# The mixer's output projection in 512-wide pieces by token halves, and cross queries moved around the memory's keys and values

## The chip, the cores and the metric

The kernel runs on one core of one Trainium2 chip. The metric is the device time of one execution in microseconds. Five engines work beside each other, each through its own list of instructions in order: TensorE (PE; PEld is its weight load), VectorE (DVE), ScalarE (ACT), GpSimd (POOL) and SyncE (SP), which here only starts transfers. They order themselves against each other by semaphores.

## What is computed

One layer of an encoder on 1024 tokens of width 1024. Three mixers (windowed attention, differential attention, a bidirectional recurrence) give one tile of 1024 features; what follows them is the part that the change touches:

```python
x = x + jnp.concatenate([o_win, o_diff, o_rwkv], axis=-1) @ w_out[l]
x = x + cross_attn(rmsnorm(x, norm_cross[l]), mem_n, x_wq[l], x_wkv[l], x_wo[l])
...
def cross_attn(h, mem_n, wq, wkv, wo):
    q = (h @ wq).reshape(b, t, X_HEADS, X_HEAD_DIM)
    kv = (mem_n @ wkv).reshape(b, m, 2, X_HEADS, X_HEAD_DIM)
    s = jnp.einsum('bqhd,bkhd->bhqk', q, kv[:, :, 0]).astype(f32) * (X_HEAD_DIM ** -0.5)
    p = jax.nn.softmax(s, axis=-1)
    o = jnp.einsum('bhqk,bkhd->bqhd', p.astype(h.dtype), kv[:, :, 1])...
    return o @ wo
```

`mem_n` is the normed memory of 256 tokens, there are 4 heads of 128, and a SwiGLU block of width 2816 and a last norm follow.

## The kernel before

Every large product is made of three matmuls on split operands: activations are kept as a rounded part HH and a rest HL, weights as WH and WL, and HH·WH, HH·WL and HL·WH are summed in PSUM.

**The weight pipeline.** Weights come in pieces of 256 KB, numbered through the whole kernel (`pieces`). SP loads piece p into one of three RAW buffers once piece p-3 has been read out; ACT rounds it to WH (`hi`, L590), POOL makes WL (`lo`, L428), and PE takes it (`take`). There are six WH/WL slots, so ACT may round piece p only when PE has finished piece p-6 (`w_used`). ACT has `hi(upto)` calls between its other work, and these calls set how far ahead of PE it gets. A piece is either 256 rows by 256 columns (`slab`) or 128 rows by 512 columns (`wide_slab`). One piece of `w_out` as a `slab` feeds 48 matmuls with 256 moving columns.

**The stage in question** is the list `jobs2` on PE: four jobs of the output projection (`wout`, each 256 output columns for all 1024 tokens, with the token tiles as stationary operand, `token_job` L1545 and following), four of the memory's keys and values (`wkv`, on the 256 memory tokens), two of the queries (`wq`, 256 features each for all tokens, `feature_job`, lines L1540 to L1543). PSUM has eight banks and the jobs take banks 0-3 and 4-7 in turn; before job j PE waits for the evacuation of job j-2.

- Ahead of job 0 the recurrence's last steps are still running; `out_ready` weaves them in between the pieces of job 0. When the mixer's tile is done (`p_y`), SP loads the residual X (eight transfers of 512 KB) between weight pieces, then the memory MX and three gain rows GBM, GBC, GBF, each spread over the partitions.
- DVE adds each `wout` job into X (`add_x`, L1415). The memory is normed (`nm`) after job 1: ACT takes the sum of squares and the root (`stat`, L596, L597), DVE scales (L1025), PE transposes (`norm_tile`, L1579), ACT rounds (`norm_hi`, L602), DVE takes the rest (`norm_lo`, L1030).
- Only when all four `wout` jobs are added can the norm of X (`n2`, eight tiles of 128 tokens) start; its tiles are transposed between pieces of the `wkv` jobs, at the places in `X_TILES`.
- The `wq` jobs follow when all tiles are normed. ACT copies each result of four banks to QC (L920), 2048 elements wide.

**The cross attention** then runs over eight tiles of 128 tokens: `scores` on PE (L2038), maximum on DVE (L1435), exponentials on ACT (L951), division on DVE (L1441, L1443), `turned` on PE (L2047), copy to CPT on ACT (L970), `values` on PE (L2056), OH on ACT (L959), OL on DVE (L1447), then the product with `x_wo` (`wo_half`) and the add (L1455). The scores of tile qb+1 are issued ahead of the turning of tile qb, so a steady tile hides its neighbour's chain; the first has no neighbour.

## Time and profile before

| | us |
|---|---|
| median of 3 runs | 1897.2 |
| lowest and highest of them | 1892.85, 1897.43 |
| the profiled execution | 1889.26 |
| its span, first to last instruction | 1887.5 |
| PE busy in the span | 1714.2 (91%) |

The profiled execution is 1.8 us longer than its span and 7.9 us (0.4%) below the median. Times within the trace are microseconds from the span's start. The stage of the change lies between 866.8 us (first matmul of the output projection) and about 1074 us (first matmul of `wo_half`). Durations of matmuls in the trace overlap: what a matmul costs in a stream is the distance from its start to that of the next.

### The profile page before, as it was taken

Reading aid. Unit: us, or ns where it says so; the run is one execution under the profiler, and the core shown is the slowest. Engines: PE = TensorE matmul, PEld = TensorE weight load, DVE = VectorE, ACT = ScalarE, POOL = GpSimd, SP = SyncE. Lnnn points to the kernel's source line nnn. Section 1 sums busy time; section 2 is a strip of 40 time slices with the busy share of each in tenths; the row PEclk is TensorE's granted clock in tenths of the full one; section 3 lists DMA queues with packets and bytes.
Section 4 is the critical chain, followed back from the end, with each engine's and each line's share of the span. In section 5 each row is a group of like instructions: output and inputs, shape, how many; then the busy total and the mean of one; then the engine's idle time right before and its main releaser. Section 6 shows DMA issues by size and latency. Waiting matters only on the chain.

```text
span 1887.5 us, 32560 instructions
## 1 busy us (share of the span) xinstructions
PE 1714.2 (91%) x13937; PEld 1429.4 (76%) x13937; DVE 728.1 (39%) x1209; ACT 651.3 (35%) x1218; POOL 544.8 (29%) x498
## 2 busy tenths in 40 slices
PE   6998999799766982989999899999999999999998
PEld 5886878688554761777997687888888888888886
DVE  3104888043175557455232263131133033213316
ACT  4224888223256433433234374211111121211212
POOL 4222662221034325325234102222222222222220
PEclk9998999899878995999999999999999999999999
DMA  5110000121000000002413101211111111111112
GB/s 185 51 60 1 1 1 1 40 61 34 17 1 6 4 4 0 4 4 75 160 49 97 34 1 51 57 50 41 55 50 46 45 51 51 44 56 48 43 45 95
DMA packets 60176, 81.20 MB, mean 43 GB/s; under 512 B 4626, under 2 KB 47792, under 8 KB 60032
## 3 DMA queue, kind: packets, MB, share of 16 engines
q1 hardware_dynamic: 59088, 76.60, 12.9%
q0 software_dynamic: 944, 2.52, 0.5%
q8 instruction: 111, 1.82, 0.4%
q14 instruction: 33, 0.27, 0.0%
HBM read 74.90 MB, written 4.19 MB: 42 GB/s over the span
## 4 chain that ended last, share of the span: by engine, by line
PE 81%; DVE 10%; ACT 5%; issue 2%; DMA 1%; POOL 1%; SPq 0%; DVEq 0%; ACTq 0%
PE PS L1540 13%; PE PS L1543 13%; PE PS L1541 13%; PE PS L1793 7%; PE PS L2137 4%; PE PS L2135 4%; PE PS L2136 4%; PE PS L1553 3%; PE PS L1555 3%; PE PS L1554 3%; PE PS L1651 3%; PE PS L1685 2%; PE PS L1857 2%; PE PS L1677 1%; PE PS L2056 1%
## 5 line engine op out<-in xcount | busy, mean ns | idle before, releaser
L428 POOL TENSOR_TENSOR WL<-RAW,WH 128x512 fp32r<-128x512 f32 x224 | 305.7, 1374 | 912.5 <-ACT WH L590 912.5
L1540 PE MATMUL PS<-HH,WH 128*128 128x512 f32 x1040 | 407.2, 391 | 9.5 <-POOL WL L428 8.1
L1541 PE MATMUL PS<-HL,WH 128*128 128x512 f32 x1040 | 406.3, 391 | 0.0
L590 ACT ACTIVATE WH<-RAW 128x512 fp32r<-128x512 f32 x224 | 138.7, 631 | 595.2 <-PE PS L1543 294.6
L1543 PE MATMUL PS<-HH,WL 128*128 128x512 f32 x1040 | 321.9, 391 | 0.0
L1540 PEld LDWEIGHTS PS<-HH,WH 128*128 128x128 f32 x1040 | 196.4, 189 | 50.7 <-issue 8.4
L1543 PEld LDWEIGHTS PS<-HH,WL 128*128 128x128 f32 x1040 | 196.2, 189 | 41.0
L1541 PEld LDWEIGHTS PS<-HL,WH 128*128 128x128 f32 x1040 | 196.3, 189 | 40.6
L1490 DVE TENSOR_TENSOR FU<-PS,ACTB 128x512 f32<-128x512 f32 x44 | 27.3, 684 | 456.9 <-PE PS L1543 456.9
L2135 PE MATMUL PS<-WH,AH 128*128 128x512 f32 x352 | 136.9, 389 | 0.0
L2136 PE MATMUL PS<-WL,AH 128*128 128x512 f32 x352 | 136.9, 389 | 0.0
L2137 PE MATMUL PS<-WH,AL 128*128 128x512 f32 x352 | 136.9, 389 | 0.0
L1517 DVE TENSOR_TENSOR X<-PS,X 128x512 f32<-128x512 f32 x160 | 105.3, 686 | 60.1 <-PE PS L2137 60.1
L1553 PE MATMUL PS<-WH,HH 128*128 128x256 f32 (+2 forms) x368 | 112.0, 304 | 6.3 <-POOL WL L428 4.1
L1555 PE MATMUL PS<-WH,HL 128*128 128x256 f32 (+2 forms) x368 | 110.8, 301 | 0.0
L1554 PE MATMUL PS<-WL,HH 128*128 128x256 f32 (+2 forms) x368 | 110.7, 301 | 0.0
L541 POOL TENSOR_TENSOR s_LT<-s_G,CN 128x256 f32<-128x256 f32 x80 | 57.6, 727 | 143.9 <-PE PS L1793 77.4
L1099 DVE CUSTOM_DVE_ANT_0 E__70<-PS,TAB 128x1024 f32<-128x1024 f32 x64 | 78.4, 1225 | 21.7 <-PE PS L1651 20.2
L1651 PE MATMUL PS<-KST,QST 128*128 128x512 f32 x256 | 79.1, 435 | 7.0 <-DVE KST L1070 7.0
L848 ACT ACTIVATE s_XQ<-PS 128x512 f32<-128x512 f32 (+1 forms) x80 | 51.1, 640 | 86.9 <-PE PS L1793 86.9
L1553 PEld LDWEIGHTS PS<-WH,HH 128*128 128x128 f32 x368 | 72.3, 196 | 9.8 <-ACT WX L590 3.0
L695 ACT ACTIVATE E__70<-E__70,SM 128x1024 f32<-128x1024 f32 x64 | 73.6, 1150 | 16.3 <-DVE SM L1099 16.0
(317 smaller groups left out, 2781.7 us busy)
## 6 DMA issues: line engine op xcount, KB each, us to landing
RAW<-in_ffn_w_gu SPq DMA_DIRECT2D x88, 256.0 KB, 2.8
RAW<-in_w_in SPq DMA_DIRECT2D x48, 256.0 KB, 2.8
RAW<-in_ffn_w_down SPq DMA_DIRECT2D x44, 256.0 KB, 2.6
XT<-in_x SPq DMA_DIRECT2D x8, 512.0 KB, 5.5
RAW<-in_w_out SPq DMA_DIRECT2D x16, 256.0 KB, 2.7
X<-in_x SPq DMA_DIRECT2D x8, 512.0 KB, 8.2
RAW<-in_x_wkv SPq DMA_DIRECT2D x16, 256.0 KB, 2.6
out_x<-FO SPq DMA_DIRECT2D x8, 512.0 KB, 2.6
```

The costliest lines, as they stand in the source:

```text
L428: pool.tensor_tensor(w_low, RAW[:, p % NRAW], w_high.bitcast(F32), ALU.subtract).then_inc(w_lo, 1)
L590: act.activation(split_at(p)[0], RAW[:, p % NRAW], ACT.Copy).then_inc(w_hi, 1)
L1540: pe.matmul(where(ct, i), wh[:, k, c], ah(kt)[:, t0:t0 + n], start=first and starts(ct, i), stop=False, skip_group_check=True)
L1541: pe.matmul(where(ct, i), wh[:, k, c], al(kt)[:, t0:t0 + n], start=False, stop=False, skip_group_check=True)
L1543: mm = pe.matmul(where(ct, i), wl[:, k, c], ah(kt)[:, t0:t0 + n], start=False, stop=last, skip_group_check=True)
L1553: pe.matmul(dst, ah(kt)[:, t], wh, start=start, stop=False, skip_group_check=True)
L1554: pe.matmul(dst, ah(kt)[:, t], wl, start=False, stop=False, skip_group_check=True)
L1555: return pe.matmul(dst, al(kt)[:, t], wh, start=False, stop=last, skip_group_check=True)
L1651: mm = pe.matmul(PS[:, 2 * c + half, :], QST[:, u // 2 % 2, part, c, P * (u % 2):P * (u % 2) + P], KST[:, h % 2, c, 512 * half:512 * half ...
L2135: pe.matmul(PS[:, bank, :], AH[:, a, t], wh, start=k == 0, stop=False, skip_group_check=True)
L2136: pe.matmul(PS[:, bank, :], AH[:, a, t], wl, start=False, stop=False, skip_group_check=True)
L2137: return pe.matmul(PS[:, bank, :], AL[:, a, t], wh, start=False, stop=k == 1, skip_group_check=True)
```

## The change

The order of the jobs becomes: four `wout` jobs, the first halves of two `wq` jobs, four `wkv` jobs, the second halves of the `wq` jobs.

- **Output projection.** A `wout` job is now 512 output columns for 4 token tiles (`out_job`, 8 pieces of `wide_slab`, 12 matmuls of 512 columns a piece). Jobs 0 and 1 make both column halves of tokens 0-511, jobs 2 and 3 of tokens 512-1023. Since each job pair walks all of `w_out`, its pieces are loaded twice: 32 pieces and not 16. The recurrence's last steps stand between the same amounts of work.
- **Norms.** X tiles 0-3 are normed inside job 2 (after pieces `X_EARLY`), the memory inside job 3 (`MEM_AT`), X tiles 4-7 inside the first `wq` halves (`X_LATE`). The statistics wait for single adds (`x_added`, four per job).
- **Queries.** `wq` is loaded twice as well (16 pieces and not 8): tokens 0-511 ahead of `wkv`, tokens 512-1023 behind it. A job fills two banks and ACT's copy is 1024 wide.
- **First cross tile.** `scores(0)` stands before the first of the last two jobs, `turned(0)` and `scores(1)` before the second. ACT's and DVE's steps for it move with them. ACT prepares the last four pieces of `x_wo` (`hi(N_LIN)`) after OH of tile 0 and ahead of the exponentials of tile 2.
- **Transfers.** SP loads seven pieces and not three before it waits for `p_y`, and puts one weight piece between any two of the other transfers. POOL makes a WL piece before each of its six HL tiles and not before each second one.
- Three semaphores are joined to one, and `x_in` becomes two, one for each token half.

```diff
@@ -215,8 +215,11 @@
-        for c0 in range(0, D, PW):
-            pieces += slab(w_out_, c0)
+        for _ in range(2):
+            for c0 in range(0, D, 512):
+                pieces += wide_slab(w_out_, c0)
+        for c0 in range(0, 512, PW):
+            pieces += slab(wq, c0)
         for c0 in range(0, 1024, PW):
             pieces += slab(wkv, c0)
         for c0 in range(0, 512, PW):
...
@@ -252,11 +255,14 @@
-        jobs2 = [("wout", i) for i in range(4)] + [("wkv", i) for i in range(4)] + [("wq", i) for i in range(2)]
-        job2_act, job2_dve = sem("job2_act"), sem("job2_dve")
+        jobs2 = ([("wout", i) for i in range(4)] + [("wq_first", i) for i in range(2)] + [("wkv", i) for i in range(4)]
+                 + [("wq_second", i) for i in range(2)])
+        JOB2_BANK = (4, 0, 4, 0, 4, 0, 4, 0, 5, 3, 4, 6)
+        Q_FIRST, KEYS, VALS, Q_SECOND = 4, 6, 8, 10
+        job2_act, x_added = sem("job2_act"), sem("x_added")
         end2, e = [], 4 * NJ
         for kind, _ in jobs2:
-            e += 4
+            e += 8 if kind == "wout" else 4
             end2.append(e)
 
         def ff0(i):
...
@@ -339,7 +349,7 @@
-        X_TILES = (1, 3, 5, 7, 9, 10, 12, 13)
+        X_EARLY, MEM_AT, X_LATE = (2, 3, 5, 6), (2, 4), (1, 3, 4, 6)
...
@@ -381,22 +391,27 @@
-            for _ in range(3):
+            for _ in range(7):
                 load(p)
                 p += 1
             sp.wait_ge(p_y, 1)
             for tt in range(NT):
-                sp.dma_start(X[:, tt], io["x"][0, tt * P:(tt + 1) * P, :]).then_inc(x_in, 16)
-                if tt % 2:
+                sp.dma_start(X[:, tt], io["x"][0, tt * P:(tt + 1) * P, :]).then_inc(x_in[tt // 4], 16)
+                if tt >= 3:
                     load(p)
                     p += 1
-            for tt in range(2):
-                sp.dma_start(MX[:, tt], io["mem"][0, tt * P:(tt + 1) * P, :]).then_inc(nm.full[tt], 16)
             sp.wait_ge(mix_lo_dve, 2)
             sp.wait_ge(mix_lo_pool, 6)
             sp.wait_ge(mix_hi, 8)
+            sp.dma_start(GBC[:, :], io["norm_cross"][0:1, :].broadcast_to([P, D])).then_inc(gain_in["mem_cross"], 16)
+            load(p)
             sp.dma_start(GBM[:, :], io["norm_mem"].rearrange("(a d) -> a d", a=1).broadcast_to([P, D])).then_inc(gain_in["mem_cross"], 16)
-            sp.dma_start(GBC[:, :], io["norm_cross"][0:1, :].broadcast_to([P, D])).then_inc(gain_in["mem_cross"], 16)
+            load(p + 1)
+            p += 2
+            for tt in range(2):
+                sp.dma_start(MX[:, tt], io["mem"][0, tt * P:(tt + 1) * P, :]).then_inc(nm.full[tt], 16)
+                load(p)
+                p += 1
...
@@ -560,10 +575,9 @@
-                if k % 2 == 0:
-                    lo(4 * NJ + k // 2)
+                lo(4 * NJ + k)
                 mix_second(k)
-            for p in range(4 * NJ + NRAW, len(pieces)):
+            for p in range(4 * NJ + 6, len(pieces)):
                 lo(p)
 
...
@@ -888,10 +902,11 @@
             act.activation(SQY[:, :, :], YY[:, :, :], ACT.Square).then_inc(p_sq, 1)
+            hi(4 * NJ + 4)
             act.wait_ge(p_mm, 3)
             act.activation(NR, PS[:, 0, 0:32], ACT.Sqrt, bias=GN_EPS, scale=1.0 / C).then_inc(p_std, 1)
             mix_first((4, 5))
-            hi(4 * NJ + NW)
+            hi(4 * NJ + 10)
             act.wait_ge(p_y, 1)
             mix_first((6, 7))
...
@@ -899,47 +914,54 @@
+            args = (lambda tt: X[:, tt], J3[:, :], AS, lambda tt: act.wait_ge(x_added, x_done(tt)))
+            for tt in range(2):
+                stat(n2, tt, *args)
+            for tt in range(4):
+                hi(p0 + 16 + X_EARLY[tt] + 6)
+                if tt + 2 < 4:
+                    stat(n2, tt + 2, *args)
+                norm_hi(n2, tt, x_hi, bank=lambda tt: 2 * (tt % 2))
...
+            for tt in range(4, NT):
+                g = X_LATE[tt - 4]
+                if tt == 6:
+                    evac2(Q_FIRST)
+                hi(p0 + 32 + g + 6)
                 if tt + 2 < NT:
                     stat(n2, tt + 2, *args)
                 norm_hi(n2, tt, x_hi, bank=lambda tt: 2 + 4 * (tt % 2))
-            evac2(7)
-            hi(WO0 + 2)
-            evac2(8)
-            hi(WO0 + 5)
-            evac2(9)
-            hi(WO0 + NW)
+            for j in range(Q_FIRST + 1, Q_SECOND):
+                hi(end2[j] + 5)
+                evac2(j)
...
@@ -958,20 +980,30 @@
             c_exps(0)
-            hi(N_LIN)
+            hi(end2[Q_SECOND] + 5)
+            evac2(Q_SECOND)
+            c_turned(0)
+            c_exps(1)
+            hi(WO0 + 4)
+            evac2(Q_SECOND + 1)
             for qb in range(NT + 2):
-                if qb + 1 < NT:
+                if 1 <= qb < NT - 1:
                     c_exps(qb + 1)
-                if qb < NT:
-                    act.wait_ge(c_tr, qb + 1)
-                    if qb >= 2:
-                        act.wait_ge(c_pv, qb - 1)
-                    act.activation(CPT[:, qb % 2, :].rearrange("p (b c) -> p b c", c=512), PS[:, 2:4, :], ACT.Copy).then_inc(c_pt, 1)
+                if 1 <= qb < NT:
+                    c_turned(qb)
                 if qb >= 2:
                     norm_hi(n3, qb - 2, x_hi, bank=lambda tt: 6)
                 if qb < NT:
                     c_first(qb)
+                if qb == 0:
+                    hi(N_LIN)
                 if qb == NT:
...
@@ -1407,27 +1439,42 @@
+            def add_x(j):
 
                 dve.wait_ge(w_used, end2[j])
+                if j >= 2:
+                    dve.wait_ge(x_in[1], 64)
                 for k in range(4):
-                    xs = X[:, 2 * k:2 * k + 2, i * PW:(i + 1) * PW]
-                    ins = TT(xs, PS[:, 4 * ((j + 1) % 2) + k, :].rearrange("p (t c) -> p t c", t=2), xs, ALU.add)
-                ins.then_inc(job2_dve, 1)
-
-            dve.wait_ge(x_in, 16 * NT)
-            add_x(0, 0)
+                    xs = X[:, 4 * (j // 2) + k, 512 * (j % 2):512 * (j % 2) + 512]
+                    TT(xs, PS[:, 4 * ((j + 1) % 2) + k, :], xs, ALU.add).then_inc(x_added, 1)
+
+            def x_norm(tts, bank):
+                scale(n2, tts[0], *x_args)
+                for tt in tts:
+                    if tt < tts[-1]:
+                        scale(n2, tt + 1, *x_args)
+                    norm_lo(n2, tt, lambda tt, b: HH[:, 4 * b:4 * b + 4, tt * P:(tt + 1) * P],
+                            lambda tt, b: HL[:, 4 * b:4 * b + 4, tt * P:(tt + 1) * P], bank)
+
+            x_args = (lambda tt: X[:, tt], lambda tt: XN2[:, tt % 2], AS, AR, GBC[:, :])
+
+            dve.wait_ge(x_in[0], 64)
+            add_x(0)
...
                  lambda tt, b: AL[:, :, :].rearrange(mt, k=4)[:, 4 * b:4 * b + 4, tt * P:(tt + 1) * P], bank=lambda tt: 4 + 2 * tt)
-            for i in range(1, 4):
-                add_x(i, i)
-            dve.wait_ge(job2_dve, 4)
-            norm(n2, lambda tt: X[:, tt], lambda tt: XN2[:, tt % 2], AS, AR, GBC[:, :], "mem_cross",
-                 lambda tt, b: HH[:, 4 * b:4 * b + 4, tt * P:(tt + 1) * P], lambda tt, b: HL[:, 4 * b:4 * b + 4, tt * P:(tt + 1) * P],
-                 bank=lambda tt: 2 + 4 * (tt % 2))
+            add_x(3)
+            dve.wait_ge(x_added, 16)
+            dve.wait_ge(nm.tr, 4)
+            x_norm((4, 5, 6, 7), lambda tt: 2 + 4 * (tt % 2))
 
             def c_row_max(qb):
                 c = slice(4 * (qb % 2), 4 * (qb % 2) + 4)
...
@@ -1983,53 +2030,43 @@
+            def out_job(j, bank, after):
+
+                for kt in range(KD):
+                    if j == 0:
+                        out_ready(kt)
+                    wh, wl = (w.rearrange("p k c -> p (k c)") for w in take())
+                    for k in range(4):
+                        mm = token_mm(PS[:, bank + k, :], wh, wl, hh, hl, kt, 4 * (j // 2) + k, kt == 0, kt == KD - 1)
+                    mm.then_inc(w_used, 1)
+                    after(kt)
+
+            def x_early(kt):
+                if kt == X_EARLY[0]:
+                    pe.wait_ge(*evac_of[1])
+                if kt in X_EARLY:
+                    norm_tile(n2, X_EARLY.index(kt), lambda tt: XN2[:, tt % 2], bank=lambda tt: 2 * (tt % 2), reuse=2)
+
+            def mem_tiles(kt):
+                if kt == MEM_AT[0]:
+                    pe.wait_ge(*evac_of[2])
+                if kt in MEM_AT:
+                    norm_tile(nm, MEM_AT.index(kt), lambda tt: XN2[:, tt], bank=lambda tt: 4 + 2 * tt)
...
@@ -2046,6 +2083,43 @@
+            for j, (kind, i) in enumerate(jobs2):
+                if j >= 2:
+                    pe.wait_ge(*evac_of[j - 2])
+                bank = JOB2_BANK[j]
+
+                def x_tile(q):
+
+                    g = 4 * i + q
+                    if g == X_LATE[0]:
+                        pe.wait_ge(*evac_of[3])
+                    if g in X_LATE:
+                        norm_tile(n2, 4 + X_LATE.index(g), lambda tt: XN2[:, tt % 2], bank=lambda tt: 2 + 4 * (tt % 2), reuse=2)
+
+                if kind == "wout":
+                    if i == 3:
+                        pe.wait_ge(n2.lo, 8)
+                    out_job(i, bank, (lambda kt: None, lambda kt: None, x_early, mem_tiles)[i])
+                    if i == 3:
+                        pe.wait_ge(nm.lo, 4)
+                elif kind == "wkv" and i < 2:
+                    feature_job(4, mh, ml, lambda ct, _: PS[:, bank, 256 * ct:256 * ct + 256], starts=lambda ct, _: ct == 0, cols=((0, 256),))
+                elif kind == "wkv":
+                    if i == 3:
+                        pe.wait_ge(n2.lo, 2 * NT)
+                    token_job(4, mh, ml, bank, nt=2)
+                elif kind == "wq_first":
+                    feature_job(4, hh, hl, lambda ct, _: PS[:, bank + ct, :], cols=((0, 512),), after=x_tile)
+                else:
+                    if i == 0:
+                        scores(0)
+                    else:
+                        turned(0)
+                        scores(1)
+                    feature_job(4, hh, hl, lambda ct, _: PS[:, bank + ct, :], cols=((512, 512),))
+
+            pe.wait_ge(*evac_of[Q_SECOND + 1])
 
             def values(qb):
                 pe.wait_ge(c_pt, qb + 1)
...
```

Where the instructions stand, in three places.

PE at the end of output job 1 before, where the memory's tiles are transposed; `[waits ...]` names the semaphores:

```order
L1555 MATMUL PS<-WH,HL 128x256
L1579 MATMUL PS<-CN,XN_118 128x128 [waits nm_xn,job2_dve]
L1579 MATMUL PS<-CN,XN_118 128x128 x7
L1579 MATMUL PS<-CN,XN_118 128x128 [waits nm_xn]
L1579 MATMUL PS<-CN,XN_118 128x128 x7
L1553 MATMUL PS<-WH,HH 128x256 [waits w_hi,w_lo,job2_dve,nm_lo]
```

PE in output job 2 of the changed kernel, where X tile 0 is transposed behind the third piece:

```order
L1602 MATMUL PS<-WH,HL 128x512
L1626 MATMUL PS<-CN,XN_118 128x128 [waits n2_xn,x_added]
L1626 MATMUL PS<-CN,XN_118 128x128 x7
L1600 MATMUL PS<-WH,HH 128x512 [waits w_lo,w_hi]
L1601 MATMUL PS<-WL,HH 128x512
```

Before, two memory tiles stood together and the next job waited for `nm_lo` right behind them; now each tile has matmuls of 512 columns on both sides.

PE at the first cross tile before:

```order
L1543 MATMUL PS<-HH,WL 128x512 x2
L2038 MATMUL PS<-KM,QC 128x256 [waits job2_act]
L2038 MATMUL PS<-KM,QC 128x256 x3
L2038 MATMUL PS<-KM,QC 128x256 [waits c_exp]
L2038 MATMUL PS<-KM,QC 128x256 x3
L2047 MATMUL PS<-CN,CP 128x128 [waits c_p]
L2047 MATMUL PS<-CN,CP 128x128 x7
L2056 MATMUL PS<-CPT,VM 128x128 [waits c_pt]
L2056 MATMUL PS<-CPT,VM 128x128 x7
```

And in the changed kernel between its last two query jobs:

```order
L1590 MATMUL PS<-HH,WL 128x512
L2084 MATMUL PS<-CN,CP 128x128 [waits c_p,job2_act]
L2084 MATMUL PS<-CN,CP 128x128 x7
L2075 MATMUL PS<-KM,QC 128x256 [waits c_exp]
L2075 MATMUL PS<-KM,QC 128x256 x3
L1587 MATMUL PS<-HH,WH 128x512 [waits w_lo,w_hi]
```

The four steps of the tile stood in a row, each with a wait; now the scores of tile 0 are one query job (48 matmuls) ahead of its turning.

ACT at the first cross tile before:

```order
L920 ACTIVATE QC<-PS 128x2048 [waits w_used]
L590 ACTIVATE WH<-RAW 128x512 [waits w_lo,w_used,raw_full0]
L951 ACT_TABLE_LOAD
L951 ACTIVATE CP,SM<-PS,SM 128x256 [waits c_max]
L951 ACTIVATE CP,SM<-PS,SM 128x256 x3
L590 ACTIVATE WY<-RAW 128x512 [waits w_used,raw_full1]
L590 ACTIVATE WY<-RAW 128x512 [waits w_used,raw_full2]
L951 ACTIVATE CP,SM<-PS,SM 128x256 [waits c_max]
```

And in the changed kernel from the last copy of the queries:

```order
L927 ACTIVATE QC<-PS 128x2x512 [waits w_used]
L981 ACTIVATE OH<-PS 128x512 [waits c_pv]
L604 ACTIVATE WH<-RAW 128x512 [waits w_lo,w_used,raw_full2]
L604 ACTIVATE WH<-RAW 128x512 [waits w_lo,w_used,raw_full0]
L604 ACTIVATE WY<-RAW 128x512 [waits w_used,raw_full1]
L604 ACTIVATE WY<-RAW 128x512 [waits w_used,raw_full2]
L973 ACTIVATE CP,SM<-PS,SM 128x256 [waits c_tr,c_max]
```

Behind the last copy of the queries, ACT now has OH of tile 0 and four weight pieces ahead of the exponentials of tile 2.

## Rows read from the trace of the kernel before

**Rows 1.** The page: busy time by engine.
```profile
PE 1714.2 (91%) x13937; PEld 1429.4 (76%) x13937; DVE 728.1 (39%) x1209; ACT 651.3 (35%) x1218; POOL 544.8 (29%) x498
```

**Rows 2.** PE's waits, 860 to 1180 us: us in total, times, longest.
```profile
PE PS L1579 <- DVE XN L1025: 5.9, 4, 2.8
PE PS L2038 <- ACT CP L951: 3.6, 1, 3.6
PE PS L2056 <- ACT CPT L970: 3.2, 1, 3.2
...
PE PS L2038 <- ACT QC L920: 2.1, 1, 2.1
PE PS L1553 <- DVE AL L1030: 1.9, 1, 1.9
PE PS L1540 <- ACT VM L918: 1.1, 1, 1.1
...
PE PS L1553 <- DVE HL L1408: 0.3, 1, 0.3
```

**Rows 3.** Windows: length, busy of PE, PEld, DVE, ACT, POOL; PEclk, DMA, GB/s.
```profile
924.00:928.00 4.00, 4.00 (x23) 4.00 (x24) 2.28 (x4) 0.00 (x0) 1.96 (x2) 0.63 0.35 115
928.00:932.00 4.00, 4.00 (x33) 4.00 (x33) 0.00 (x0) 0.46 (x1) 0.00 (x0) 0.94 0.05 16
1061.00:1069.00 8.00, 4.64 (x17) 3.65 (x17) 3.78 (x6) 3.96 (x12) 3.22 (x2) 0.75 0.23 66
1069.00:1074.00 5.00, 5.00 (x25) 4.76 (x26) 1.11 (x2) 0.60 (x1) 0.00 (x0) 0.72 0.01 3
```

**Rows 4.** PE's timeline, two streams: start us, duration us, instruction.
```profile
876.24 0.28 PE L1553 MATMUL PS<-WH,HH 128*128 128x256 f32 x1
...
881.51 0.28 PE L1555 MATMUL PS<-WH,HL 128*128 128x256 f32 x1
...
1159.29 0.39 PE L2107 MATMUL PS<-HL,WH 128*128 128x512 f32 x1
...
1166.78 0.39 PE L2107 MATMUL PS<-HL,WH 128*128 128x512 f32 x1
```

**Rows 5.** Timeline of ACT, POOL, SP; last, transfers by tile, median us to landing.
```profile
1009.20 1.66 ACT L590 ACTIVATE WH<-RAW 128x512 fp32r<-128x512 f32 x3
1014.06 0.63 ACT L590 ACTIVATE WH<-RAW 128x512 fp32r<-128x512 f32 x1 [3.20 <-DMA RAW<-in_x_wq]
...
1014.76 1.29 POOL L428 TENSOR_TENSOR WL<-RAW,WH 128x512 fp32r<-128x512 f32 x1 [1.09 <-ACT WH L590]
...
869.04 2.29 POOL L428 TENSOR_TENSOR WL<-RAW,WH 128x512 fp32r<-128x512 f32 x1
...
888.57 0.38 SPq L358 DMA_DIRECT2D RAW<-in_w_out  x1
...
894.87 0.63 ACT L590 ACTIVATE WH<-RAW 128x512 fp32r<-128x512 f32 x1 [5.20 <-DMA RAW<-in_w_out]
898.12 0.63 ACT L590 ACTIVATE WH<-RAW 128x512 fp32r<-128x512 f32 x1 [2.62 <-DMA RAW<-in_w_out]
...
RAW<-in_w_out SPq DMA_DIRECT2D x10, 256.0 KB, 7.1
```

**Rows 6.** Groups of DVE, then ACT, 970 to 1010 us: busy us, mean ns.
```profile
L1025 DVE SCALAR_TENSOR_TENSOR XN<-X,SM,GBC 128x1024 f32<-128x1024 f32 x8 | 13.6, 1701 | 0.3
L1415 DVE TENSOR_TENSOR X<-PS,X 128x512 f32<-128x512 f32 x4 | 2.5, 683 | 20.6 <-PE PS L1555 20.6
...
L596 ACT ACTIVATE JN<-X 128x1024 f32<-128x1024 f32 x8 | 8.4, 1048 | 13.4 <-DVE X L1415 13.4
```

**Rows 7.** Timeline of ACT and DVE at the first cross tile.
```profile
1053.59 1.88 ACT L920 ACTIVATE QC<-PS 128x2048 f32<-128x2048 f32 x1 [4.76 <-PE PS L1543]
...
1061.33 1.23 DVE L1443 TENSOR_TENSOR CP<-CP,SM 128x1024 f32<-128x1024 f32 x1
...
1067.83 1.03 ACT L970 ACTIVATE CPT<-PS 128x1024 f32<-128x1024 f32 x1
```

127 lines of the change are left out of this document (53 added, 74 removed).

## The prediction

> **What bounds the kernel now.** I read the page first: PE is busy for 91% of the span, the next engine for 39% [rows 1]. So PE's own work and the holes in it set the time, and what ACT, DVE, POOL and SP do costs only where PE waits for it. The second view is the list of PE's waits from the last steps of the recurrence to the feed-forward block. In the stage that the change rewrites seven of them stand: 5.9 us for X tiles not yet scaled (DVE XN), 1.9 us for the memory's rest AL behind output job 1, 1.1 us for the last copy of the values VM, 0.3 us for the mixer's HL, and around the first cross tile 2.1 us for QC, 3.6 us for its exponentials and 3.2 us for CPT [rows 2]: 18.1 us. The third view is the table of windows. After two of these holes the granted clock falls, from 2.4 GHz towards 1.2: to 0.63 and 0.94 in 924 to 932 us, behind the wait for AL, and to 0.75 and 0.72 from 1061 to 1074 us, behind the wait for the exponentials [rows 3]. The fourth view is PE's timeline, for what one matmul of each width costs in a stream.
>
> **The change, part by part.**
>
> *Wider output projection.* From 876.24 to 881.51 us there are 44 steps from one matmul of 256 columns to the next, at full clock: 0.120 us each. From 1159.29 to 1166.78 us there are 33 steps at 512 columns: 0.227 us each [rows 4]. Before there are 4 jobs of 192 matmuls, 768 x 0.120 = 92.2 us; now 4 jobs of 96, 384 x 0.227 = 87.2 us. Saved: 5.0 us, all on PE's path. Nothing of the product is computed twice; only loads and conversions are. By that the saving would be 83.8 - 82.9 = 1.0 us; the trace has 13 ns and not 2.5 ns above the columns at both widths and decides for the sum.
>
> *Norms inside the jobs.* Before, X could not be normed until all four output jobs were added; then eight tiles had to go through ACT, DVE and PE within the 16 short `wkv` pieces, 12 matmuls of 256 columns or 1.44 us each. A tile takes a scaling of 1.70 us in the mean on DVE and 1.05 us for the square on ACT [rows 6], beside the rounding, the rest and up to two weight pieces, so they came late. Now the closest two tiles (behind pieces 2 and 3) have 12 x 0.227 = 2.7 us and one transposing of about 1 us between them, and the first two are scaled ahead into the two XN buffers; other neighbours have twice as much. For tile 0: job 1 ends, DVE adds one tile in 0.68 us, ACT squares in 1.05 us, DVE finishes its four adds (2.7 us) and scales in 1.3 to 2.2 us; PE comes to the tile after three pieces, 8.2 us. That leaves 3 us. Tile 4 is tighter, with two pieces (5.4 us) against 2.7 us of adds and 1.3 to 2.2 us of scaling: 0.5 to 1.4 us left. The memory's tiles have matmuls around them in job 3, and the wait for `nm_lo` comes three pieces (8.2 us) later. So I take out all of 5.9, 1.9 and 1.1 us (the copy of VM now has a whole query job behind it), and the 0.3 us for HL: the pieces ahead of the last two are narrower in time by 0.3 us a pair, which brings the steps to `p_y` forward, and the last two now wait each for its own HL tile and not for both. One wait is added: job 3 waits for all of X tiles 0 to 3 to be rounded, behind tile 3's transposing and one piece (2.7 us); ACT and DVE need about 2 us. I price it at 0, up to 1 us; behind it on PE stands all of job 3.
>
> *Clock.* With the hole behind job 1 gone, the stretch 924 to 932 us gains 4 x 0.37 + 4 x 0.06 = 1.7 us. For 1061 to 1074 us I count busy time alone: 4.64 x 0.25 + 5.0 x 0.28 = 2.6 us [rows 3]. Together 4.3 us.
>
> *First cross tile.* The chain scores, maximum, exponentials, division, turning took PE's two waits of 3.6 and 3.2 us [rows 2]. It ran from the end of QC's copy at 1053.59 + 1.88 us to the end of the division at 1061.33 + 1.23 us: 7.1 us [rows 7]. In its new place 48 matmuls of 512 columns cover it, 10.9 us, and another such job covers the copy to CPT (1.03 us) and tile 1's chain. The cover is 3.8 us longer than the chain; if ACT were held by weight pieces for longer, the wait would come back from there. I take out 6.8 us. The wait for the last QC stays, with half the size: 1.88 us of copy for 2048 elements [rows 7] becomes about 1.0, as the copy of 1024 elements to CPT shows, and the hole 2.1 becomes 1.2 us. So 0.9 of it is won.
>
> *What is late next.* `hi(N_LIN)` puts four weight pieces on ACT between OH of tile 0 and the exponentials of tile 2. The fourth needs a RAW buffer that is freed only when POOL has made the first: 4.86 us pass from rounding a piece to rounding the piece that comes next in the same buffer (1009.20 to 1014.06 us) [rows 5]. ACT is thus held for about 5 us from the end of `values(0)`, while the exponentials could start after 3.4 us of it. They and CPT stand ahead of `values(1)`, so I price it at 1.1 us, from 0 to 3 us.
>
> *Feed.* 24 more pieces mean 24 x 0.63 us on ACT, 24 x 1.29 us on POOL and 6.3 MB of transfers, all on engines that PE does not wait for as long as the pace holds. PE now takes a piece of the output projection every 2.7 us (5.8 before). The pipeline can turn a buffer in 4.86 us, and there are three: one piece per 1.6 us. With POOL's slowest conversion of 2.29 us and not 1.29 it is 5.9 / 3 = 2.0 us [rows 5]. Both are below 2.7. The `wkv` pieces now take 1.44 us each with no tiles between: 16 x (1.62 - 1.44) = 3 us of deficit, which six slots (8.6 us) absorb. The tight place is the load of X: the first four tiles (2.1 MB) stand in SP's queue ahead of piece 10. The first piece issued behind two X tiles left SP at 888.57 us and was rounded at 894.87, 6.3 us later; the median of ten pieces in that stretch was 7.1 us [rows 5]. Two X tiles more are 1.05 MB, about 2.6 us at the pace of that queue (1.31 MB in 3.3 us, from this piece to the next). That makes piece 10 ready at 888.6 + 6.3 + 2.6 + 0.63 + 1.29 = 899.4 us. PE needs it two pieces after the end of job 0, which I expect at 895 us: 900.5. I price the feed at 0, up to 6 us (below). ACT's extra rounding ahead of `p_std` and POOL's three extra WL pieces among the HL tiles end before PE comes to them, by about 4 us.
>
> *Sum.* 5.0 + 18.1 + 4.3 - 1.2 (rest of the QC wait) - 1.1 (exponentials of tile 2) = 25.1 us. The profiled execution of 1889.3 us would become 1864.2. It lies 7.9 us below the median of the runs; from the median of 1897.2 the same gain gives **1872.1 us**. The cross loop from its second tile and the feed-forward block are unchanged.
>
> **The rivals.**
>
> *A, forecast:* 22 to 29 us are won, 1868 to 1875 us.
>
> *B, the feed is late behind X.* If pieces land 7.1 us after their issue as long as the queue is full, a buffer turns in 7.1 + 0.63 + 1.29 = 9.0 us, 3.0 us a piece against 2.7. For the eleven pieces 10 to 20 that is 3.3 us, and about 1 us for piece 10 itself: 1876.5 us; with a landing of 8 us it is 6 us, 1878. For it speaks the landing time [rows 5], against it that behind the first four X tiles only one other transfer stands between two pieces, and that six pieces are ready when the stretch begins.
>
> *C, the first cross tile's chain is not covered*, since ACT reaches the exponentials late. Then 6.8 us and the 2.6 us of clock come back: 1881.5 us. The order on ACT speaks against it: nothing but one short copy stands between the values' pieces and the exponentials.
>
> *D, the wide matmuls give only 1.0 us.* This would be so if the 13 ns above the columns were not paid per matmul when the token tiles are the stationary operand at this width: 1876 us. The rows at 512 columns are those of the same operand kinds, which speaks against it. It is what the page named above would give.
>
> *E, slower.* The whole stage runs at the pace of the buffers: if the slow turn of B held for all 48 long pieces (32 of the output, 16 of the queries) and ACT's and POOL's other work in order lengthened it to 10.5 us, that is 3.5 us a piece. The loss equals the gain at 2.7 + 25.1 / 48 = 3.2 us a piece; at 3.5 the result is 48 x 0.3 = 14 us slower than before, 1911 us. The pieces at 1.6 us in the same kernel without X in the queue speak against it.
>
> *F, no change:* waits moved one for one to other places, 1897 us; nothing in the profile speaks for it but that every wait of the stage was touched.
>
> **Chances.** A 0.66, B 0.15, C 0.07, D 0.04, E 0.04, F 0.04. The predicted time is A's, 1872 us. The range takes in B and C and A's upper gain counted from the profiled execution (1889.3 - 29 = 1860): 1860 to 1884 us. About 0.3% (6 us) is what a measurement of this kernel can tell from no change. Faster by more than that: 0.92 (A to D); within: 0.04 (F); slower: 0.04 (E).
>
> **What would show it.** In the changed profile, from 866.8 us on: output jobs as streams at 0.227 us a matmul, with no wait for WL or WH; job 0 ending about 2 us earlier; no wait for XN, AL or VM; the granted clock at 1.00 up to `values`; `turned(0)` without a wait; one wait of 1.2 us for QC; and the first `wo_half` 26 to 28 us earlier than 1074 us. A wait for WL in job 1 would show B, one for CP before `turned(0)` C, a step of 0.238 us at 512 columns D. The prediction is wrong if waits for weights add up to more than 10 us, or if the clock falls in the new order.

## The result and the profile after

The changed kernel takes 1860.8 us (median of 4, 1855.9 to 1867.1), the kernel before beside it 1897.3 us (1892.9 to 1897.9): a ratio of 0.9835, 95% interval 0.981 to 0.986. The forecast was 1872 us, range 1860 to 1884. The direction is right, and the time lies at the low end of the range, 0.8 us inside it. The profiled execution took 1856.6 us, against 1889.3 before. Its page answers to [rows 1]:

```profile
PE 1698.7 (92%) x13553; PEld 1399.5 (75%) x13553; DVE 732.8 (40%) x1209; ACT 666.6 (36%) x1244; POOL 579.8 (31%) x522
```

PE has 384 matmuls and 15.5 us of busy time less, ACT 15 us and POOL 35 us more, for the 24 weight pieces more. To say where the time came from, the traces have to be compared stage by stage. The stage below runs from the last matmul of the recurrence's square sums, behind which the first output matmul follows, to the first matmul of the feed-forward block. PE's timeline before:

```profile
864.80 2.15 PE L1701 MATMUL PS<-CN,SQY 128*128 128x2 f32 x18
866.81 0.39 PE L1553 MATMUL PS<-WH,HH 128*128 128x256 f32 x1
...
1159.06 0.40 PE L2106 MATMUL PS<-HH,WH 128*128 128x512 f32 x1
```

and after:

```profile
858.86 1.81 PE L1748 MATMUL PS<-CN,SQY 128*128 128x2 f32 x15
860.53 0.57 PE L1600 MATMUL PS<-WH,HH 128*128 128x512 f32 x1
...
1125.83 0.40 PE L2179 MATMUL PS<-HH,WH 128*128 128x512 f32 x1
```

The stage took 1159.1 - 866.7 = 292.4 us, and takes 1125.8 - 860.4 = 265.4 us. That is 27.0 us of the 32.7 between the two profiled spans (1887.5 and 1854.8). Another 6.3 us lie ahead of the stage, where the change only joins semaphores; what they are is the first question of the experiments.

PE's waits in the stage, after (us in total, times, longest), against [rows 2]:

```profile
PE PS L1600 <- DVE OL L1494: 2.8, 2, 1.4
PE PS L1600 <- DVE X L1502: 2.8, 5, 0.6
PE PS L2130 <- ACT QC L927: 1.1, 1, 1.1
PE PS L1600 <- POOL WY L443: 0.4, 1, 0.4
PE PS L2130 <- ACT CPT L987: 0.3, 1, 0.3
```

The first two belong to the cross loop and stood there before with the same size (2.8 and 2.8 us). The waits for XN, AL, VM, HL and CP are gone. All waits together fell from 23.7 to 7.4 us. The remaining three stand at the first cross tile. The windows at the start of the output jobs and at the first cross tile (columns as in [rows 3]):

```profile
860.50:864.50 4.00, 4.00 (x13) 3.14 (x13) 3.52 (x2) 3.12 (x5) 4.00 (x3) 0.57 0.22 66
864.50:868.50 4.00, 4.00 (x23) 3.38 (x22) 0.30 (x1) 0.63 (x1) 4.00 (x3) 1.00 0.20 70
...
1032.00:1036.00 4.00, 2.89 (x14) 2.07 (x13) 0.00 (x0) 1.02 (x1) 0.36 (x1) 1.00 0.41 134
1036.00:1040.00 4.00, 4.00 (x27) 3.67 (x28) 1.02 (x2) 2.06 (x4) 0.87 (x1) 1.00 0.00 0
```

The first 4 us of the output projection have a mean granted clock of 0.57 in both kernels' profiles (it is at its lower level for most of them); behind them it is 1.00 to the end of the stage. The wait for QC (1032 to 1036 us) does not bring it down.

The feed: X tiles and pieces on SP, then the first pieces on ACT (timelines, start us, duration us), against [rows 5]:

```profile
881.04 1.75 SPq L399 DMA_DIRECT2D X<-in_x  x4
882.89 0.68 SPq L368 DMA_DIRECT2D RAW<-in_w_out  x1
...
889.48 0.63 ACT L604 ACTIVATE WH<-RAW 128x512 fp32r<-128x512 f32 x1 [6.43 <-DMA RAW<-in_w_out]
891.76 0.63 ACT L604 ACTIVATE WH<-RAW 128x512 fp32r<-128x512 f32 x1 [1.64 <-DMA RAW<-in_w_out]
```

The piece behind the four X tiles is rounded 6.6 us after its issue, and the next nine pieces follow in 2.3 us each in the mean (1.8 to 3.3), below the 2.7 us in which PE uses one.

### The profile page after: what moved, and what is told of

It reads as the page before. It is cut to its first block, busy times and chain, and to the rows that moved or that the text cites. A ratio compares the mean times of both kernels' runs of the same rounds, so it can differ in the third digit from the quotient of the medians.

```text
span 1854.8 us, 31941 instructions
## 1 busy us (share of the span) xinstructions
PE 1698.7 (92%) x13553; PEld 1399.5 (75%) x13553; DVE 732.8 (40%) x1209; ACT 666.6 (36%) x1244; POOL 579.8 (31%) x522
## 4 chain that ended last, share of the span: by engine, by line
PE 83%; DVE 9%; ACT 4%; issue 2%; DMA 1%; POOL 1%; SPq 0%; ACTq 0%; DVEq 0%
PE PS L1587 13%; PE PS L1590 13%; PE PS L1588 13%; PE PS L1840 7%; PE PS L2210 4%; PE PS L2209 4%; PE PS L2208 4%; PE PS L1600 3%; PE PS L1602 3%; PE PS L1601 3%; PE PS L1698 3%; PE PS L1732 2%; PE PS L1904 2%; PE PS L1724 1%; PE PS L1626 1%
## 5 line engine op out<-in xcount | busy, mean ns | idle before, releaser
L443 POOL TENSOR_TENSOR WL<-RAW,WH 128x512 fp32r<-128x512 f32 x248 | 341.0, 1384 | 858.2 <-ACT WH L604 857.7
L604 ACT ACTIVATE WH<-RAW 128x512 fp32r<-128x512 f32 x248 | 153.7, 631 | 569.4 <-PE PS L1590 270.4
L1590 PE MATMUL PS<-HH,WL 128*128 128x512 f32 x1040 | 326.9, 391 | 0.0
L1537 DVE TENSOR_TENSOR FU<-PS,ACTB 128x512 f32<-128x512 f32 x44 | 27.3, 683 | 456.9 <-PE PS L1590 456.9
L1600 PE MATMUL PS<-WH,HH 128*128 128x512 f32 (+1 forms) x240 | 89.4, 373 | 2.6 <-POOL WL L443 2.5
L1601 PE MATMUL PS<-WL,HH 128*128 128x512 f32 (+1 forms) x240 | 87.8, 366 | 0.0
L1602 PE MATMUL PS<-WH,HL 128*128 128x512 f32 (+1 forms) x240 | 87.8, 366 | 0.0
L2210 PEld LDWEIGHTS PS<-WH,AL 128*128 128x128 f32 x352 | 66.1, 188 | 13.7
## 6 DMA issues: line engine op xcount, KB each, us to landing
RAW<-in_ffn_w_gu SPq DMA_DIRECT2D x88, 256.0 KB, 2.8
RAW<-in_w_in SPq DMA_DIRECT2D x48, 256.0 KB, 2.7
RAW<-in_ffn_w_down SPq DMA_DIRECT2D x44, 256.0 KB, 2.6
RAW<-in_w_out SPq DMA_DIRECT2D x32, 256.0 KB, 2.6
RAW<-in_x_wq SPq DMA_DIRECT2D x16, 256.0 KB, 2.7
RAW<-in_x_wkv SPq DMA_DIRECT2D x16, 256.0 KB, 2.6
```

Source lines behind the costliest of these rows:

```text
L443: pool.tensor_tensor(w_low, RAW[:, p % NRAW], w_high.bitcast(F32), ALU.subtract).then_inc(w_lo, 1)
L604: act.activation(split_at(p)[0], RAW[:, p % NRAW], ACT.Copy).then_inc(w_hi, 1)
L1590: mm = pe.matmul(where(ct, i), wl[:, k, c], ah(kt)[:, t0:t0 + n], start=False, stop=last, skip_group_check=True)
L1600: pe.matmul(dst, ah(kt)[:, t], wh, start=start, stop=False, skip_group_check=True)
L1601: pe.matmul(dst, ah(kt)[:, t], wl, start=False, stop=False, skip_group_check=True)
L1602: return pe.matmul(dst, al(kt)[:, t], wh, start=False, stop=last, skip_group_check=True)
```

## The experiments

All ratios are to the kernel before, run on the same chip in the same set; brackets hold the 95% interval. The first two rows of the table are the forecast's and the result's own runs. Behind them there were three sets, r1, r2 and r3; the kernel before had a median of 1896.8 us in r1, 1891.6 in r2, 1891.9 in r3. "Start" is the last matmul of the square sums in the profiled execution, "stage" the stretch from there to the feed-forward block.

| kernel | median us | ratio | start | stage |
|---|---|---|---|---|
| before (forecast's profile) | 1897.2 | 1 | 866.7 | 292.4 |
| after (result's profile) | 1860.8 | 0.9835 [0.981, 0.986] | 860.4 | 265.4 |
| r1_before | 1890.8 | 0.9974 [0.9956, 0.9993] | 872.0 | 293.6 |
| r1_after | 1868.8 | 0.9855 [0.9832, 0.9877] | 871.7 | 266.2 |
| r1_crossback | 1877.0 | 0.9889 [0.9863, 0.9915] | 862.7 | 274.6 |
| r1_narrow | 1871.2 | 0.9864 [0.984, 0.9889] | 865.5 | 269.7 |
| r2_memhole | 1866.4 | 0.9866 [0.9834, 0.9899] | 868.0 | 267.0 |
| r2_latenorm | 1857.7 | 0.9816 [0.9782, 0.985] | 872.7 | 264.7 |
| r2_slowlo | 1870.3 | 0.988 [0.9847, 0.9913] | 872.2 | 269.2 |
| r2_sems | 1888.1 | 0.9982 [0.9959, 1.0005] | 859.5 | 292.1 |
| r3_after | 1863.5 | 0.9844 [0.9819, 0.9869] | 867.3 | 264.7 |
| r3_first | 1861.4 | 0.9833 [0.9807, 0.9858] | 866.3 | 263.0 |
| r3_both | 1856.7 | 0.9809 [0.9783, 0.9835] | 862.9 | 262.9 |
| r3_shift | 1895.2 | 1.0021 [1.0005, 1.0037] | 872.7 | 297.0 |

The stage repeats well: the changed kernel has 265.4, 266.2 and 264.7 us, mean 265.4; the old stage has 292.4, 293.6 and, with the joined semaphores, 292.1, mean 292.7. The start does not repeat: it lies anywhere between 859.5 and 872.7 us with either kernel. So the stage is the measure for effects of one or two microseconds. For the whole time r1_before gives the measure: it is the kernel before against itself, in the same set, and its median came out 6.0 us lower, with an interval (0.9956 to 0.9993) that leaves out 1. A difference of whole times of 6 us or less therefore proves nothing here, even where its interval leaves out 1.

### Both kernels again

First both kernels once more, unchanged.

> The kernel before, unedited, timed against itself: what the measurement gives for no change, and a second trace of it. Both theories: ratio 1.000 +- 0.003. Theory 1: the output projection may start anywhere between 858 and 870 us in its trace, the stage from there to the first feed-forward matmul stays at 292 us +- 1. Theory 2: it starts near 866.8 us again.

> The changed kernel once more, unedited, for more rounds and a second trace. The profiled executions differ by 32.7 us in span: 26.9 us lie between the first matmul of the output projection and the first of the feed-forward block, 6.3 us ahead of that stage, where nothing was rewritten. Theory 1 (the 6.3 us are a matter of the clock's course in the recurrence and differ from execution to execution, in either kernel): over more rounds the gain shrinks towards the stage's 27 us, ratio about 0.986, and the new trace has its own upstream time, with the stage again 265 us +- 1. Theory 2 (the change moves the upstream part): the ratio stays at 0.981 and the output projection starts near 860.5 us again.

Measured: the start is 872.0 us in the kernel before and 871.7 in the changed one; the stage 293.6 and 266.2. Where do 5 to 11 us go ahead of the stage? Windows of the kernel before in the forecast's profile:

```profile
500.00:600.00 100.00, 67.66 (x407) 50.15 (x405) 58.73 (x142) 56.86 (x159) 37.19 (x23) 0.79 0.01 3
600.00:700.00 100.00, 87.26 (x2924) 70.02 (x2928) 52.11 (x135) 39.33 (x71) 28.80 (x40) 0.98 0.02 4
```

of the same kernel in this run:

```profile
500.00:600.00 100.00, 68.76 (x438) 52.54 (x439) 56.23 (x142) 56.75 (x159) 37.25 (x23) 0.77 0.01 3
600.00:700.00 100.00, 88.79 (x2904) 71.14 (x2904) 51.14 (x132) 39.44 (x72) 28.90 (x40) 0.94 0.02 4
```

and of the changed kernel in the result's profile:

```profile
500.00:600.00 100.00, 67.88 (x509) 49.98 (x507) 60.21 (x148) 57.72 (x161) 38.01 (x24) 0.82 0.01 3
600.00:700.00 100.00, 87.33 (x2939) 70.39 (x2934) 51.57 (x135) 38.94 (x70) 28.16 (x39) 0.98 0.02 4
700.00:760.00 60.00, 25.27 (x477) 16.91 (x479) 42.48 (x39) 19.57 (x25) 28.01 (x15) 0.72 0.00 1
```

The same code runs at a mean granted clock of 0.77 to 0.82 from 500 to 600 us, and at 0.98 or 0.94 from 600 to 700 us. The profiles with 0.77 and 0.94 start the stage at 872.0 (before) and 871.7 us (changed), those with 0.79 and 0.98 at 866.7 (before) and 866.3 us (r3_first), those with 0.82 and 0.98 at 860.4 (changed) and 859.5 us (r2_sems). Like clocks give like starts, whichever kernel it is. The waits of PE there have the same names and nearly the same sizes in all of them (36.9 us for SM, 9.7 to 11.7 us for WT, 7.0 to 7.1 us for s_Q). So the start goes with the clock's course in the recurrence, not with the change. Why the clock takes one course or another was not tested.

### The joined semaphores

The rival for those 6 us was the one edit ahead of the stage: three semaphores joined into one.

```diff
-            dve.wait_ge(tab_in, 16)
+            dve.wait_ge(tables_in, 16)
...
-            dve.wait_ge(wb_in, 16)
+            dve.wait_ge(tables_in, 32)
...
-                    dve.wait_ge(masks_in, 16)
+                    dve.wait_ge(tables_in, 48)
```

> The kernel before with nothing of the change but the three joined semaphores (tables_in), which is the only edit that touches instructions ahead of the output projection's first pieces. In four traces of kernels of either kind the sums of SQY ended at 866.7, 872.0 (before), 860.4, 871.7 (changed) us. Theory (the start of the stage moves with the clock's course, not with the code): somewhere from 858 to 873 us, stage 292 to 294 us, ratio 1.000 +- 0.004. Rival (the joined semaphores save time upstream): a start at 862 us or earlier and a ratio below 0.996.

Measured: a ratio of 0.9982, whose interval holds 1, and a stage of 292.1 us. The start was 859.5 us, the earliest of all. Taken alone that would have spoken for the rival, and the interval, which reaches down to 0.9959, does not exclude 6 us. But the changed kernel has the joined semaphores too and started at 871.7 us in r1_after, and r2_latenorm, which has them as well, at 872.7 us. In r1 and r3 the changed kernel is 28.0 and 28.4 us below the kernel before (22.1 us below r1_before), and the stage alone accounts for 27.3 us. So 6 us ahead of the stage are not a gain of every execution, and the first pair of profiles differs in the clock's course as well; an effect of one or two microseconds could not be seen.

### The output jobs narrow again

The changed kernel, with each matmul of 512 columns cut into two of 256, in the same jobs.

```diff
-                        mm = token_mm(PS[:, bank + k, :], wh, wl, ...)
+                        for c in (slice(0, 256), slice(256, 512)):
+                            mm = token_mm(PS[:, bank + k, c], wh[:, c], wl[:, c], ...)
```

> The changed kernel with every matmul of the output projection split into two of 256 columns; pieces, order, banks and waits as changed. My theory (a price of 13 ns per matmul above its columns): output jobs at 0.120 us a matmul, 5.0 us slower in all. Rival (2.5 ns per matmul, the rest hidden elsewhere): 1.0 us slower. Twice as many weight loads could also cost more than in the kernel before: then above 6 us.

Measured: stage 269.7 us, 3.5, 4.3 and 5.0 above the three profiles of the changed kernel (r1_after, the result's, r3_after). No new wait appears. The streams step by 0.120 and 0.227 us, as in the kernel before. PE's timeline of the narrow kernel:

```profile
905.05 0.28 PE L1600 MATMUL PS<-WH,HH 128*128 128x256 f32 x1
905.17 0.28 PE L1601 MATMUL PS<-WL,HH 128*128 128x256 f32 x1
```

and of the changed kernel, in the same job:

```profile
898.06 0.39 PE L1600 MATMUL PS<-WH,HH 128*128 128x512 f32 x1
898.28 0.39 PE L1601 MATMUL PS<-WL,HH 128*128 128x512 f32 x1
```

The smallest of the three differences, 3.5 us, is against r1_after, which ran the start of its stage at a lower clock: 0.50 in the first 4 us, and in the next 4 us

```profile
875.70:879.70 4.00, 4.00 (x14) 3.14 (x13) 0.00 (x0) 0.63 (x1) 4.00 (x4) 0.70 0.18 66
```

where r1_narrow, the result's profile and r3_after have 0.57 to 0.63, then 0.94 to 1.00. That is 1.5 us of clock which r1_narrow did not lose. With the clock and the waits taken out (the table in the section on the prediction), the narrow matmuls cost 4.5 to 4.8 us; the steps would give 5.0 us. The rival with 1.0 us falls.

### The first cross tile back in its old place

The changed kernel, with `scores(0)`, `turned(0)` and `scores(1)` behind the query jobs, and ACT's steps for them where they stood before.

```diff
-                    if i == 0:
-                        scores(0)
-                    else:
-                        turned(0)
-                        scores(1)
...
+            scores(0)
             for qb in range(NT + 1):
-                if 1 <= qb < NT - 1:
+                if qb + 1 < NT:
                     scores(qb + 1)
```

> The changed kernel with the first cross tile put back behind the query jobs: scores(0), scores(1) and turned(0) on PE, and ACT's steps for them, stand in the order of before; all else as changed. By my sum this gives back the two waits of 6.8 us, 2.6 us of clock and 0.8 us of the price on tile 2: 9 to 10 us slower than the changed kernel, with waits of PE for the exponentials (3.6 us) and CPT (3.2 us) and a granted clock below 0.8 behind them. Rival (the chain of tile 0 was cheap because the clock alone made it look long): under 5 us.

Measured: stage 274.6 us, 8.4, 9.2 and 9.9 above the three profiles of the changed kernel. PE's waits of this kernel:

```profile
PE PS L2073 <- ACT CP L973: 3.6, 1, 3.6
PE PS L2123 <- ACT CPT L987: 2.9, 1, 2.9
...
PE PS L2073 <- ACT QC L927: 1.1, 1, 1.1
```

and its windows at that place:

```profile
1038.00:1042.00 4.00, 2.50 (x8) 2.05 (x9) 1.40 (x2) 2.49 (x9) 1.96 (x1) 0.79 0.21 66
1042.00:1046.00 4.00, 2.05 (x10) 1.60 (x8) 1.41 (x3) 1.97 (x9) 1.27 (x2) 0.78 0.52 131
1046.00:1050.00 4.00, 3.07 (x15) 3.08 (x16) 1.39 (x2) 0.87 (x1) 0.00 (x0) 0.64 0.00 0
1050.00:1054.00 4.00, 4.00 (x19) 3.47 (x19) 2.09 (x3) 0.76 (x2) 0.00 (x0) 0.93 0.01 4
```

Waits of 7.6 us against 1.8 are 5.8 us. The clock takes 2.50 x 0.21 + 2.05 x 0.22 + 3.07 x 0.36 + 4.00 x 0.07 = 2.4 us of busy time; windows of 1 us, which blur less of it, give 3.3 us. Together 8.2 to 9.1 us. This part of the change carries a third of the gain, and it is the cover of the chain and the clock behind it that pay.

### A hole behind the output job

In my sum, 1.7 us of clock hung on the hole behind job 1. This kernel has both memory tiles behind piece 7 of job 3, with nothing between them and the wait for AL.

```diff
-        X_EARLY, MEM_AT, X_LATE = (2, 3, 5, 6), (2, 4), (1, 3, 4, 6)
+        X_EARLY, MEM_AT, X_LATE = (2, 3, 5, 6), (7, 7), (1, 3, 4, 6)
...
-                    norm_tile(nm, MEM_AT.index(kt), ...)
+                    for tt in range(2):
+                        norm_tile(nm, tt, ...)
```

> The changed kernel with both memory tiles transposed behind the last piece of output job 3, and the next job's wait for nm_lo right behind them, as it stood behind job 1 before. The stage (first matmul of the output projection to first of the feed-forward block) takes 265.4 and 266.2 us in two traces of the changed kernel. My theory (a hole on PE costs itself and a spell at the lower clock after it): the stage becomes 3 to 5 us longer, about 2 to 2.5 us of wait for AL and up to 2 us of clock, seen as a granted clock below 1.00 in the 8 us behind it. Rival (the clock fell before for another reason, the hole costs only itself): 2 to 2.5 us and the clock stays at 1.00.

Measured: the wait is back, and the clock stays, as the rival had it and not my theory. PE's waits, then the windows around it:

```profile
PE PS L1587 <- DVE AL L1062: 1.9, 1, 1.9
```

```profile
966.00:970.00 4.00, 2.10 (x18) 1.82 (x16) 3.00 (x5) 2.06 (x4) 0.00 (x0) 1.00 0.24 66
970.00:974.00 4.00, 4.00 (x20) 3.28 (x19) 3.89 (x8) 3.82 (x9) 0.62 (x1) 1.00 0.00 0
```

The stage is 267.0 us, 1.6 above the changed kernel's mean: the wait itself and no more. In the kernel before and in r2_sems, the wait of the same 1.9 us behind job 1 was followed by a low clock in all three profiles (0.63 in [rows 3], 0.70 and 0.73 in the other two). But r3_shift, whose instructions are the same up to there, has the same 1.9 us behind job 1, and then:

```profile
932.00:936.00 4.00, 4.00 (x36) 4.00 (x35) 1.36 (x3) 0.00 (x0) 1.05 (x1) 1.00 0.39 131
```

In the kernel with slow conversions below, a wait of 2.1 us was followed by 0.78 and 0.79. So a hole of 2 us can cost its own length or nearly twice that, and with the same code and the same wait it does one in one execution and the other in another. What decides it was not found; the place behind job 1 alone does not.

### The late X tiles within the short pieces

My reason for the waits for XN was that the short pieces of keys and values cannot cover a tile's norm. This kernel puts X tiles 4 to 7 behind pieces 1, 3, 5 and 7 of exactly these pieces, and leaves the first query jobs bare.

```diff
-        X_EARLY, MEM_AT, X_LATE = (2, 3, 5, 6), (2, 4), (1, 3, 4, 6)
+        X_EARLY, MEM_AT, X_LATE = (2, 3, 5, 6), (2, 4), (1, 3, 5, 7)
...
-                    feature_job(4, mh, ml, ..., cols=((0, 256),))
+                    feature_job(4, mh, ml, ..., cols=((0, 256),), after=x_tile)
...
-                    feature_job(4, hh, hl, ..., cols=((0, 512),), after=x_tile)
+                    feature_job(4, hh, hl, ..., cols=((0, 512),))
```

> The changed kernel with X tiles 4 to 7 transposed between the short pieces of the keys' and values' jobs (behind pieces 1, 3, 5 and 7 of them), as all eight were before, and not between the long pieces of the first query halves. My sum put 5.9 us of waits for XN on eight such tiles. Theory (the short pieces are the cause: two of them last 2.9 us, a tile's round through ACT and DVE about 3.7): 1 to 3 us of waits for XN come back, and since ACT and POOL are then shared between tiles and pieces at 1.44 us each, PE also waits for weights; stage 2 to 5 us longer. Rival (before, the tiles were late because all started from one late point, the end of the fourth job): no wait, stage 265 to 266 us.

Measured: no wait for XN at all, and a stage of 264.7 us, no longer than that of the changed kernel (264.7 to 266.2). My theory missed; the rival holds. Its waits up to the cross loop are these two:

```profile
PE PS L2133 <- ACT QC L927: 1.1, 1, 1.1
PE PS L2133 <- ACT CPT L990: 0.3, 1, 0.3
```

The short pieces alone are not the cause. Here the first two of the tiles were scaled 20 us before PE came to them, and only four tiles go through the stretch, not eight.

### The old kernel, tiles two pieces later

Then what made the old waits? There PE waited 2.8 us at tile 0, and 1.8, 0.8 and 0.6 us at tiles 5, 6 and 7 (the total of 5.9 in [rows 2]). The last experiment moves the tiles in the kernel before.

```diff
-        X_TILES = (1, 3, 5, 7, 9, 10, 12, 13)
+        X_TILES = (3, 5, 7, 9, 11, 12, 13, 14)
```

> The kernel before, with the eight X tiles' transposings behind pieces 3, 5, 7, 9, 11, 12, 13 and 14 of the sixteen short ones and not 1, 3, 5, 7, 9, 10, 12 and 13. It asks what the 5.9 us of waits for XN came from. In the kernel before, the waits were 2.8 us for tile 0, and 1.8, 0.8 and 0.6 us for tiles 5, 6 and 7. Theory 1 (only the first is due to the late common start, the others to the round of one tile through DVE, PE and ACT, about 4 to 5 us, which two short pieces and a transposing just cover and one doesn't): the wait for tile 0 goes, those of the last tiles grow to about 4.0 us in all, and as the last tile is scaled at the same time, the stage is 1.5 to 2 us shorter, 290.5 to 292. Rival 1 (all of it is the late start): no wait for XN at all and the stage 5 to 6 us shorter, 287 us. Rival 2 (nothing but the rate of the round counts): the last tile comes out as late as before and what PE saved is waited for at the query jobs, for HL: the stage is unchanged, 292.4 to 293.6 us.

Measured: a stage of 297.0 us: all three expectations missed. (The ratio of 1.0021 [1.0005, 1.0037] is within what r1_before shows for no change.) PE's waits of this kernel in the wkv jobs:

```profile
PE PS L1579 <- DVE XN L1025: 5.2, 5, 1.8
PE PS L1540 <- POOL WL L428: 1.4, 1, 1.4
PE PS L1540 <- ACT WH L590: 1.3, 1, 1.3
```

Tile 0's wait went, as theory 1 had it, but the others came to 5.2 us, and PE now waits for weights as well. ACT's waits there tell why:

```profile
ACT JN L596 <- DVE X L1415: 13.4, 1, 13.4
ACT WH L590 <- DMA RAW<-in_x_wkv: 7.7, 3, 4.0
```

In the kernel before, the second of these is 3.7 us. ACT's list has, for each tile, the weight pieces ahead of the tile's rounding, and then the rounding that DVE needs before it may scale the tile after next. A tile's place in PE's list sets how many pieces ACT must round first. Placed later, the tiles stand behind pieces that have not landed, and the round through PE, ACT and DVE takes 4.6 us a tile (983.1 to 1015.3 us for seven steps) where it took 3.9 (977.5 to 1004.7). The clock fell to 0.58 behind one of these waits:

```profile
1011.00:1015.00 4.00, 3.68 (x19) 3.68 (x20) 3.40 (x5) 3.26 (x8) 3.31 (x3) 0.58 0.19 66
```

From the first `wkv` matmul to the first one of `scores` the stretch takes 87.7 us (977.19 to 1064.9), against 84.0 and 83.9 in the two profiles of the kernel before. Of these 3.8 us, 1.2 are more idle time of PE, 1.7 the clock behind that wait, and the rest is busy time at full clock. The 0.5 us that remain of the 4.3 above the old stage's mean lie outside the stretch, mainly in the clock: 1.2 us more than before at the start, 1.7 us less behind job 1, and 0.5 to 1.8 us more at the first cross tile, where no instruction was moved.

So the old waits had two sources: the late common start at tile 0, 2.8 us, and the round of eight tiles that shares ACT with the pieces, 3.1 us. The first is shown by its going; the second rests on the rows of this run, and no run changed ACT's order alone.

### POOL's conversion twice

For the room in the feed: POOL makes the WL half of pieces 8 to 31 of the output projection (jobs 1 to 3) twice in a row, into the same place.

```diff
+                if 4 * NJ + 8 <= p < 4 * NJ + 32:
+                    link(pool.tensor_tensor(w_low, RAW[:, p % NRAW], w_high.bitcast(F32), ALU.subtract))
                 pool.tensor_tensor(w_low, RAW[:, p % NRAW], w_high.bitcast(F32), ALU.subtract).then_inc(w_lo, 1)
```

> The changed kernel with POOL making the WL of 24 pieces of the output projection (9 to 32) twice, 2.6 us and not 1.3, so a piece costs POOL nearly what PE takes for it (2.7 us) and a buffer turns in about 6 us and not 4.9. It measures how much room the feed has. Theory (the feed has room: three buffers, six slots): 0 to 2 us longer, with few short waits for WL. Rival B of the prediction (the feed is at its edge behind X's load): over 5 us longer, with waits for WL in output job 1.

Measured: stage 269.2 us, 3.8 above the mean. One wait is new, and behind it the clock is low for 8 us; PE's waits, then the windows:

```profile
PE PS L1602 <- issue: 2.1, 1, 2.1
```

```profile
948.00:952.00 4.00, 1.87 (x5) 1.41 (x5) 3.06 (x6) 3.94 (x10) 3.84 (x4) 0.78 0.32 95
952.00:956.00 4.00, 4.00 (x15) 3.22 (x15) 3.93 (x6) 1.60 (x3) 3.92 (x3) 0.79 0.32 104
```

24 conversions more, 31 us of POOL's time at 1.29 us each, cost 3.8 us, more than the 0 to 2 us of my theory and less than the 5 us of rival B; 1.6 us of it are the clock behind the wait. The feed has room where the change put its 24 pieces, though not much beyond: the trace gives no name to the wait, and that it is for a weight buffer is my reading.

### The rest of the waits, and both improvements together

Two kernels go beyond the change. The first starts the values of tile 0 when the first of the two late query copies is done, and rounds one piece more ahead of the second copy.

```diff
-            hi(WO0 + 4)
+            hi(WO0 + 5)
             evac2(Q_SECOND + 1)
...
-            pe.wait_ge(*evac_of[Q_SECOND + 1])
+            pe.wait_ge(*evac_of[Q_SECOND])
...
+                if qb == 2:
+                    pe.wait_ge(*evac_of[Q_SECOND + 1])
```

> The changed kernel, in which the first cross tile's values wait only for the copy of the first of the two last query jobs; the wait for the second copy stands ahead of the first feed-forward tile's transposing, and the rounding of one weight piece is moved ahead of that copy on ACT. Three waits of PE stand there in the changed kernel: 1.1 us for QC, 0.37 us for a weight buffer of POOL and 0.35 us for CPT. Theory 1 (they are waits of ACT's order and the end of the stage hangs on them): all three go, the stage is 1.5 to 1.8 us shorter, 263.6 to 264.7 us, time 1.5 us under the changed kernel, inside what can be told. Rival 1 (the late piece or the late copy is now waited for in another place: the second tile's turning waits for its probabilities, since ACT makes its exponentials behind one piece more): a wait for CP or CPT of about 1 us comes in and the stage stays at 265.4 to 266.2. Rival 2 (the scores of tile 2 overtake the second copy, which covers queries that they read): cannot show, since that wait is kept behind them only where nothing reads the copied part.

The second has this and the edits of r2_latenorm.

> The previous kernel's edit together with that of the kernel with late norms (X tiles 4 to 7 normed within the short pieces of the memory's keys and values, in place of the first query jobs). Late norms alone had a stage of 264.7 us against 265.4 and 266.2, no wait for XN. Theory 1 (the two edits lie in different places and add): stage 262.5 to 264 us, 2 to 3 us under the changed kernel, a ratio to before of 0.981 to 0.984. Rival (the second edit's gain needs ACT to be ahead, which late norms take away: ACT then reaches the exponentials of the first tile later): stage as with late norms alone, 264 to 265 us, and a wait for CP or QC of about 1 us.

Beside them the changed kernel once more:

> The changed kernel once more, as the measure for the other three of this set. The two profiled executions so far had 265.4 and 266.2 us from the end of the recurrence's square sums to the first matmul of the feed-forward block (called the stage), before 292.4 and 293.6. Theory 1 (the change is worth what the stage lost, 27.0 to 27.4 us; what a median differs beyond that is where the clock stands upstream): stage 265 to 266.5 us, time 26 to 28 us under before, a ratio near 0.9855. Rival (the change also speeds something upstream, 6 us, as the first pair of profiles had it): the stage begins 6 us earlier than before's 866.7 us again, the time is 33 to 36 us under before, a ratio of 0.981 to 0.983.

Measured: r3_first has none of the three waits left, and none came in their place; the stage is 263.0 us, 1.7 below the changed kernel in the same set, as theory 1 had it. r3_both has 262.9 us. That lies in the range of its theory 1, but r3_first alone has 263.0: the two edits do not add, since late norms took away nothing that still stood in PE's path. Its median of 1856.7 us is the lowest of its set (1863.5 for the changed kernel), but only 1.8 us of that lie in the stage; the start was 4.4 us earlier. Against the kernel before it is 0.9809 [0.9783, 0.9835]; that it beats the changed kernel by 1.8 us is in the traces, and the intervals of the two ratios overlap.

## Why the prediction was right, step by step

**The sum.** 25.1 us were forecast, 27.3 us is what the stage lost (292.7 - 265.4, means of three). The forecast's 1872.1 us stands 11.3 us above the measured median. Of this, 2.2 us is the sum. The other 9 us are where the executions fell. The medians of the changed kernel were 1860.8 (result), 1868.8 (r1) and 1863.5 us (r3), those of the kernel before beside them 1897.3, 1896.8 and 1891.9: the result's pair has the largest distance, 36.5 us, the other two have 28.0 and 28.4 us. So the miss of 11 us is mostly chance, and so is how close the time lies to the end of the range: the range held by 0.8 us, and its lower end stood at 1860 only because I had counted the largest gain from the profiled execution. The step that failed is not in the sum but in its use: I took a gain worked out in one stage, and put it on the median of a time that wanders by more than the terms I argued about. That wandering was in no term; the profiled execution's 7.9 us below the median was a sign of it.

**An account of the stage.** Cut into windows of 1 us, each stage can be split into the time in which PE is idle, the busy time that the clock took (busy time x (1 - granted clock), summed), and the rest, which is the work at full clock. The split is worked out from the traces; the clock's part is an estimate.

| kernel | stage | idle | clock | rest |
|---|---|---|---|---|
| before | 292.4 | 23.7 | 6.6 | 262.2 |
| r1_before | 293.6 | 24.0 | 7.6 | 262.0 |
| r2_sems | 292.1 | 23.4 | 6.6 | 262.1 |
| after | 265.4 | 7.4 | 1.7 | 256.3 |
| r1_after | 266.2 | 7.0 | 3.2 | 256.0 |
| r3_after | 264.7 | 7.0 | 1.7 | 256.0 |
| r1_narrow | 269.7 | 7.2 | 1.7 | 260.8 |
| r1_crossback | 274.6 | 13.2 | 5.1 | 256.4 |
| r3_shift | 297.0 | 24.3 | 9.5 | 263.2 |

Most of what a stage of one kernel differs by between executions is in the column of the clock. From before to after the idle time fell by 16.3 us, the clock's part by 4.9 us and the rest by 5.9 us.

**Wider output projection**, 5.0 us forecast: 4.5 to 4.8 measured (the rest of r1_narrow against that of the three profiles of the changed kernel), with the forecast's steps of 0.120 and 0.227 us in both traces. The term was right. Job 0 ends 28.8 us after the square sums, against 30.4 before: 1.6 us earlier, forecast about 2. The figure of the Trainium skill (TensorE: Matmul & The Clock Gate, section Back-to-back issue gap), which stands there for an isolated matmul and not for a stream, and by which I had rival D at 1.0 us, is below what the run shows; the measurement decides.

**The waits**, 18.1 - 1.2 - 1.1 = 15.8 us forecast: 16.3 us measured (23.7 to 7.4 us). Every wait I took out is gone. The new wait for QC is 1.1 us (forecast 1.2). The first `wo_half` comes 28.1 us earlier in the stage (178.9 us into it, 207.0 before), where the forecast had 26 to 28; against the span's start it is 34.4 us earlier, with the 6.3 us ahead of the stage. For the four pieces of `hi(N_LIN)` I had priced 1.1 us, and the trace has 0.37 us for WY and 0.35 us for CPT; the stage from the first `wo_half` on is 1.2 us longer than before (86.5 against 85.3). ACT's timeline shows the mechanism as forecast, the last piece held up by its transfer and the exponentials behind it:

```profile
1043.72 0.63 ACT L604 ACTIVATE WY<-RAW 128x512 fp32r<-128x512 f32 x1 [3.62 <-DMA RAW<-in_x_wo]
1044.26 0.46 ACT L973 ACTIVATE CP<-PS,SM 128x256 f32<-128x256 f32 x1
```

The added wait for tiles 0 to 3 cost nothing, as priced. My reason for the XN waits was wrong in one half: not the length of the pieces, but the common start and a round that shares ACT with pieces still on their way. The change removes both, so the price held.

**The clock**, 4.3 us forecast: 4.9 us by the table, 1.7 behind job 1 and 3.1 at the first cross tile. Both profiles lose the same 1.7 us at the start of the stage. The forecast's windows of 8 and 5 us at the first cross tile mixed idle with busy time; windows of 4 us show more of it:

```profile
1060.70:1064.70 4.00, 3.57 (x10) 2.82 (x11) 1.55 (x3) 1.42 (x4) 3.02 (x2) 0.61 0.00 0
1064.70:1068.70 4.00, 0.98 (x8) 0.74 (x6) 1.93 (x4) 2.69 (x9) 0.20 (x1) 0.93 0.47 131
1068.70:1072.70 4.00, 3.79 (x19) 3.74 (x20) 0.72 (x1) 0.49 (x2) 0.00 (x0) 0.61 0.01 4
```

3.57 x 0.39 + 0.98 x 0.07 + 3.79 x 0.39 = 2.9 us. The term was right in kind and 0.6 us too small.

**What is left.** The rest fell by 5.9 us, and the width explains 4.5 to 4.8 of them. 1.1 to 1.4 us stay open. A candidate is what a stop costs beside its wait: the last matmul ahead of one is busy for 0.28 or 0.39 us and not only its step of 0.120 or 0.227, 0.16 us more. The stage had ten such stops at the places of [rows 2] and has three now: an estimate of 7 x 0.16 = 1.1 us. No run tests it.

**First cross tile.** With its clock the forecast had 6.8 + 2.6 - 1.1 = 8.3 us for the part that r1_crossback undoes; that run gives 8.4 to 9.9. Rival C falls.

**The feed**, priced at 0: right. No wait for WH or WL in the output and query jobs. Piece 10 was ready at 889.48 + 0.63 + 1.29 = 891.4 us, 31.0 us into the stage, and PE came to it two pieces after job 0, 34.3 us into it; the forecast had 32.7 and 33.8. Rival B had a buffer turning in 9.0 us; the pieces behind X came every 2.3 us, so three buffers turned in 7.0. Rival E would have needed 3.2 us a piece for the gain to be lost. r2_slowlo shows that the feed can come to limit PE: with 31 us more work on POOL a first wait appeared.

## What to carry to other kernels

Compare two kernels over the stretch that the change touches, between two instructions that both have: here it repeats within 1.5 us, while its start moves by 13 us with the clock in code that nobody edited. A chain of small steps between two jobs costs PE its length and, in most profiles here, the clock behind it too; inside a job that does not need it, it cost nothing, as long as its first steps are done before PE arrives. Before moving a step in one engine's list, read what the other engines have in order ahead of it: in the old kernel the same tiles two pieces later made the stage longer, since ACT had more weight pieces to wait for first. Time a kernel against itself as well: here the same code differed by 6.0 us, with an interval that left out 1.

## What the runs showed of the hardware

The recurrence, the same instructions with the same waits, was run at a mean granted clock of 0.93 (r3_both, r1_crossback, r3_shift), 0.94 (r1_before, r1_after, r2_slowlo, r2_latenorm) or 0.98 (the other profiles) between 600 and 700 us, and the stage behind it started at 859.5 to 872.7 us over the profiled executions of all kernels. Two kernels' single profiles cannot be told apart by less than that ahead of the stage.

A stop of PE of 1.9 us left the clock at 1.00 in two kernels (r2_memhole, r3_shift) and one of the same length was followed by 0.63 in the kernel before [rows 3], with the same instructions ahead of it as in r3_shift; one of 2.1 us was followed by 0.78 and 0.79 (r2_slowlo).
